# A weight load of the expert stage issued as two transfers: rows 0 to 119 and rows 120 to 127

## The chip, the cores and the metric

The kernel runs on one core of a Trainium2 chip. Its time is the device time in microseconds (us). The median of several runs is taken.

The core has a matrix engine (PE in the profile, TensorE), a vector engine (DVE), a scalar engine (ACT), GpSimd (POOL) and a queue engine (SP). SP only issues transfers here. Sixteen DMA engines carry them. A transfer raises its semaphore by 16 in all when it has landed.

## The reference

A decoder trunk of two layers on 256 tokens of width 1024, in float32. Each layer has a token mixer (attention, pooling, short convolution), a cross-attention and a channel mixer. The channel mixer of the second layer matters here: each token goes to the best 2 of 8 experts.

```python
for e in range(N_EXPERTS):                       # 8 experts, D_FF_EXPERT = 3584
    out = out + gates[:, e:e + 1] * swiglu(xt, w13[e], w2[e])
# swiglu: g, u = split(x @ w13); (silu(g) * u) @ w2
```

An expert's weights are 1024 x 7168 and 3584 x 1024 float32 numbers. They are read once each.

## The kernel before

The expert stage works through items. Item i takes the tokens of one expert (up to 64 in odd items, up to 96 in even ones) through that expert's weights. With these inputs there are eight items; further items, for experts with more tokens, stand in a loop that isn't entered.

The weights of an item come in 42 units (`ITEM_UNITS`), 336 in all. A unit is 128 rows of 2048 float32 numbers, so 8 KB a row and 1 MB a unit. In HBM it is contiguous. Units are laid in a ring of 20 slots (`RING`): six buffers of `raw`, and 14 older tensors that the stage before has finished with, under names such as `slot_bias` and `slot_yT_hi`. Unit number u of the whole stage goes to slot u mod 20. Slot 19 is the tensor `slot_xT_lo`.

SP issues the loads in the order of the units. Before each it waits (`hold`, L402) until PE has read the unit that lay in the slot before, 20 units earlier. `load_unit` (L446) then issues one transfer, which raises `in{slot}` by 16. PE waits in `arrived` (L1907) for `units.landed(u)` on that semaphore, reads the unit with matmuls (`product`, L1860) straight from its slot, and raises `units_read`. The rows of tokens are held as weights of the matmul and the unit is streamed, so a unit costs PE more time in an even item than in an odd one.

Items run in turn: even items with the `mid_up` and `mid_down` forms (L1860, 96 rows, in groups of 32), odd items with `few_up` and `few_down` (64 rows). The last item, number 7, is an odd one. After its last unit come a scaling, the sum back to the tokens (`back`, L1834 and L1835), the final norm, and the output.

An earlier transfer plays a part in the prediction. At L427 four transfers of 32 rows each fill `bias` from the tensor `skew` in HBM.

Of the kernel before, what the change touches and what calls it, by code (L numbers as in the profile page):

```python
# [18 lines left out]
P = 128  # L19
# [28 lines left out]
SPLIT = 3  # L48
RING = 20
OVER_RING = 14  # L50

LAYER_UNITS = 22
DENSE_UNITS = 33
# [124 lines left out]
class Stream:  # L178
# [9 lines left out]
    def landed(self, u):  # L188
        return (self.rounds + ((self.off + u) // RAW + 1)) * 16
# [12 lines left out]
def units_from(first):  # L202
    return Stream(first, first // RAW, first % RAW)
# [6 lines left out]
def layer_stream(l):  # L210
    return units_from(l * (LAYER_UNITS + DENSE_UNITS))

class Units:
# [6 lines left out]
        return (self.off + u) % self.ring  # L221

    def landed(self, u):
        return self.rounds * 16 + ((self.off + u) // self.ring + 1) * 16

    def read(self, u):
        return self.first + (u + 1)
# [5 lines left out]
def item_units(i):  # L233
    u = i * ITEM_UNITS
    return Units(u, u // RING, u % RING, RING)

def over_units(k):

    rounds = (NE * ITEM_UNITS - OVER_RING) // RING + 1  # L240
    return Units(k * ITEM_UNITS + NE * ITEM_UNITS, k * (ITEM_UNITS // OVER_RING) + rounds, 0, OVER_RING)

# [6 lines left out]
def _build(nc, io, ctx):  # L249
# [12 lines left out]
    def sem(name):  # L262
        if name not in sems:
            sems[name] = ctx.enter_context(nc.semaphore(name))
        return sems[name]
# [97 lines left out]
    slots = [raw[:, (MOE_BASE + n) % RAW, :] for n in range(RAW)]  # L363
# [34 lines left out]
    def hold(eng, name, count):  # L398

        eng.wait_ge(sem(name), count)
        eng.sem_inc(sem("held"), 1)  # L402

    @block.sync
    def _(sp):
        def load(st, u, src, width=UNIT):
            hold(sp, f"free{st.slot(u)}", st.freed(u))
            sp.dma_start(raw[:, st.slot(u), 0:width], src).then_inc(sem(f"raw{st.slot(u)}"), 16)

        for t in range(NT):
            sp.dma_start(x_tiles[t], io["x"][0, t * P:(t + 1) * P, :]).then_inc(sem(f"x_in{t}"), 16)
        sp.dma_start(g_row[:, :], io["mix_norm_g"][0].rearrange("(o d) -> o d", o=1).broadcast_to([P, D]))\
            .then_inc(sem("first_gain_in"), 16)
        sp.dma_start(ident, io["mats"][:, 0, :]).then_inc(sem("ident_in"), 16)

        for l in range(DEPTH):
            st = layer_stream(l)
            for u in range(LAYER_UNITS):
                load(st, u, io["layer_units"][l, u])  # L420
                if l == 0 and u == RAW - 1:
                    sp.wait_ge(sem("skew_rows"), 1)
                    sp.dma_start(skew.ap(), skew_rows.unsqueeze(1).broadcast_to([HEADS, SKEW_P, SKEW_W]))\
                        .then_inc(sem("skew_out"), 16)
                    sp.wait_ge(sem("skew_out"), 16)
                    for a in range(0, P, SKEW_P):
                        sp.dma_start(bias[a:a + SKEW_P, :, :],  # L427
                                     bass.AP(skew, P - 1 - a, [[SKEW_W - 1, SKEW_P], [SKEW_P * SKEW_W, HEADS], [1, T]]))\
                            .then_inc(sem("bias_in"), 16)
            if l < 1:  # L430
                for u in range(DENSE_UNITS):
                    load(st, LAYER_UNITS + u, io["dense_units"][u])

        moe = io["moe_units"]
        last = layer_stream(DEPTH - 1)

        def unit_done(u):
            return "unit_used", last.upto(u) + 2 * SPLIT

        room = [(f"free{units_from(MOE_BASE).slot(n)}", units_from(MOE_BASE).freed(n)) for n in range(RAW)]  # L440
        room += [("logits", DEPTH * HEADS), ("xlogits_mm", DEPTH * XHEADS), unit_done(19)]
        room += [unit_done(19)] * 2 + [unit_done(20)] * 2 + [unit_done(21)] * 4 + [("router_mm", 1)] * 3

        def load_unit(units, u, src):
            slot = units.slot(u)
            sp.dma_start(slots[slot], src).then_inc(sem(f"in{slot}"), 16)  # L446

        for u in range(ITEM_UNITS):
            if u < RING:
                hold(sp, *room[u])  # L450
            else:
                hold(sp, "units_read", item_units(0).room(u))
            load_unit(item_units(0), u, moe[u])
        sp.wait_ge(sem("info_ready"), 1)
        n_items = sp.value_load(info[0:1, 0:1], min_val=NE, max_val=ITEMS)
        for i in range(1, NE):
            e = sp.value_load(info[0:1, i + 1:i + 2], min_val=0, max_val=NE - 1)
            for u in range(ITEM_UNITS):
                hold(sp, "units_read", item_units(i).room(u))
                load_unit(item_units(i), u, moe[e * ITEM_UNITS + u])  # L460
        with sp.Fori(0, OVER) as k:
            with sp.If(n_items > k + NE):
                e = sp.value_load(info[0:1, bass.ds(k + (NE + 1), 1)], min_val=0, max_val=NE - 1)
                hold(sp, "units_read", k * ITEM_UNITS + NE * ITEM_UNITS)
                for u in range(ITEM_UNITS):
                    if u >= OVER_RING:
                        hold(sp, "units_read", over_units(k).room(u))
                    load_unit(over_units(k), u, moe[e * ITEM_UNITS + u])
            sp.nop()
        for t in range(NT):  # L470
            for half in range(2):
                s = slice(half * 512, (half + 1) * 512)
                sp.wait_ge(sem("xn_ready"), 4 * (3 * DEPTH + 1) + 2 * t + half + 1)
                sp.dma_start(io["out"][0, t * P:(t + 1) * P, s], xn[:, t, s]).then_inc(sem("out_done"), 16)
        sp.wait_ge(sem("out_done"), 32 * NT)
# [1543 lines left out]
```

## Time and profile before

| | |
|---|---|
| median of 3 runs | 1376.26 us (1376.21 to 1376.49) |
| the profiled execution | 1376.58 us |
| its span, first to last instruction | 1374.7 us |
| PE busy | 1347.6 us, 98% of the span |
| transfers | 444.58 MB, mean 323 GB/s |

The page tells the busy time of each engine, then the span in 40 equal slices, in which a digit is the busy share in tenths. The DMA line is the mean over the 16 DMA engines. A chain follows what ended last back through what released it. Windows give the same for any stretch that one asks for.

### The profile page before, as it was taken

The numbers are of one execution on the slowest core, as the hardware profiler recorded it, in microseconds if no ns is written. First come the engines' busy times: TensorE is split into PE (matmuls) and PEld (weight loads), VectorE is DVE, ScalarE is ACT, GpSimd is POOL, SyncE is SP. The second block draws the span as 40 slices with busy tenths as digits, with TensorE's granted clock in tenths as the row PEclk, the third lists the DMA queues.
The fourth block names the chain that finished last, engine by engine and source line by source line (L and its number), as shares of the span: only waits on it lengthen the run. The fifth ranks groups of instructions, "written<-read, shape, count | busy, mean of one in ns | idle before, by whom it ended". The sixth has DMA issues, their size and how long they took to land.

```text
span 1374.7 us, 29896 instructions
## 1 busy us (share of the span) xinstructions
PE 1347.6 (98%) x13281; PEld 1063.0 (77%) x13281; DVE 411.8 (30%) x761; ACT 321.8 (23%) x587; POOL 13.9 (1%) x27
## 2 busy tenths in 40 slices
PE   9999999999999999999999999999999999999994
PEld 6989888888798888888557888557888557887542
DVE  6677555554747753200100100100100100100102
ACT  6445454443644533000001000001000000000001
POOL 1000000000000000000000000000000000000000
PEclk9999999999999999999999999999999999999998
DMA  8826345555543569999999999999999999999992
GB/s 317 314 96 223 124 169 184 184 187 190 191 154 123 185 250 399 413 378 352 409 421 420 420 419 419 420 421 419 420 420 420 420 421 420 420 420 420 421 420 116
DMA packets 63901, 444.58 MB, mean 323 GB/s; under 512 B 7262, under 2 KB 8686, under 8 KB 10905
## 3 DMA queue, kind: packets, MB, share of 16 engines
q1 hardware_dynamic: 61976, 437.22, 79.7%
q0 software_dynamic: 1792, 5.41, 1.1%
q8 instruction: 106, 1.74, 0.5%
q14 instruction: 27, 0.21, 0.0%
HBM read 441.16 MB, written 1.44 MB: 322 GB/s over the span
## 4 chain that ended last, share of the span: by engine, by line
PE 93%; DVE 3%; DMA 2%; issue 1%; ACT 1%; SPq 0%; DVEq 0%; ACTq 0%
PE bank L1860 52%; PE bank L1440 10%; PE bank L1442 10%; PE bank L1441 10%; PE bank L1824 2%; DMA slot_yT_hi<-in_moe_units 2%; PE bank L1922 2%; PE bank L1834 1%; PE bank L1528 1%; PE bank L1482 1%; PE bank L1835 1%; DVE w_lo L826 1%; PE bank L1649 1%; PE bank L1569 1%; PE bank L1632 1%
## 5 line engine op out<-in xcount | busy, mean ns | idle before, releaser
L1373 DVE TENSOR_TENSOR hidden<-hidden,bank 128x384 f32<-128x384 f32 (+1 forms) x56 | 27.3, 487 | 587.7 <-ACT hidden L786 587.7
L826 DVE TENSOR_TENSOR w_lo<-raw,w_hi 128x1024 fp32r<-128x1024 f32 x154 | 181.1, 1219 | 42.8 <-ACT w_hi L524 41.3
L524 ACT ACTIVATE w_hi<-raw 128x1024 fp32r<-128x1024 f32 x154 | 154.5, 1057 | 40.5 <-PE bank L1442 40.5
L786 ACT ACTIVATE hidden<-bank 128x384 f32<-128x384 f32 (+1 forms) x56 | 24.5, 437 | 365.5 <-PE bank L1860 365.5
L1860 PE MATMUL bank<-raw,mid_x 128*32 128x384 f32 (+1 forms) x1632 | 92.8, 380 | 1.0 <-ACT mid_x L760 1.0
L1860 PEld LDWEIGHTS bank<-raw,mid_x 128*32 128x32 f32 x1632 | 88.7, 110 | 4.5 <-issue 3.1
L779 ACT ACTIVATE hT<-bank 128x384 f32<-128x384 f32 (+1 forms) x56 | 24.5, 437 | 288.5 <-PE bank L1922 288.5
L1440 PE MATMUL bank<-xT_hi,w_hi 128*128 128x256 f32 x320 | 91.8, 287 | 0.0
L1441 PE MATMUL bank<-xT_lo,w_hi 128*128 128x256 f32 x320 | 90.5, 283 | 0.0
L1442 PE MATMUL bank<-xT_hi,w_lo 128*128 128x256 f32 x320 | 90.4, 283 | 0.0
L1440 PE MATMUL bank<-w_hi,xT_hi 128*128 128x512 f32 (+1 forms) x224 | 85.2, 380 | 1.1 <-DVE w_lo L826 0.6
L1442 PE MATMUL bank<-w_hi,xT_lo 128*128 128x512 f32 (+1 forms) x224 | 83.9, 375 | 0.0
L1441 PE MATMUL bank<-w_lo,xT_hi 128*128 128x512 f32 (+1 forms) x224 | 83.8, 374 | 0.0
L1860 PE MATMUL bank<-raw,hT 128*32 128x256 f32 (+2 forms) x792 | 81.8, 476 | 0.0
L1440 PE MATMUL bank<-w_hi,yT_hi 128*128 128x512 f32 x184 | 73.3, 398 | 1.3 <-DVE yT_lo L838 0.8
L1442 PE MATMUL bank<-w_hi,yT_lo 128*128 128x512 f32 x184 | 71.8, 390 | 0.0
L1441 PE MATMUL bank<-w_lo,yT_hi 128*128 128x512 f32 x184 | 71.7, 390 | 0.0
L1860 PEld LDWEIGHTS bank<-raw,hT 128*32 128x32 f32 (+1 forms) x792 | 43.4, 115 | 29.2 <-issue 15.4
L1440 PEld LDWEIGHTS bank<-xT_hi,w_hi 128*128 128x128 f32 x320 | 61.3, 192 | 0.7 <-issue 0.7
L1441 PEld LDWEIGHTS bank<-xT_lo,w_hi 128*128 128x128 f32 x320 | 61.3, 192 | 0.1
L1442 PEld LDWEIGHTS bank<-xT_hi,w_lo 128*128 128x128 f32 x320 | 61.3, 191 | 0.0
L1860 PE MATMUL bank<-raw,few_x 128*64 128x256 f32 x512 | 59.3, 382 | 0.5 <-DMA raw<-in_moe_units 0.5
(326 smaller groups left out, 2100.1 us busy)
## 6 DMA issues: line engine op xcount, KB each, us to landing
raw<-in_moe_units SPq DMA_DIRECT2D x102, 1024.0 KB, 24.9
slot_w_hi<-in_moe_units SPq DMA_DIRECT2D x51, 1024.0 KB, 25.8
slot_w_lo<-in_moe_units SPq DMA_DIRECT2D x51, 1024.0 KB, 26.0
raw<-in_layer_units SPq DMA_DIRECT2D x44, 1024.0 KB, 5.1
raw<-in_dense_units SPq DMA_DIRECT2D x33, 1024.0 KB, 4.9
slot_bias<-in_moe_units SPq DMA_DIRECT2D x17, 1024.0 KB, 26.0
slot_qk<-in_moe_units SPq DMA_DIRECT2D x17, 1024.0 KB, 26.4
slot_memT_lo<-in_moe_units SPq DMA_DIRECT2D x17, 1024.0 KB, 26.7
```

Source lines behind the costliest of these rows:

```text
L524: act.activation(w_hi[:, st.split(u), half, :], raw[:, st.slot(u), half * n:(half + 1) * n], ACT.Copy)\
L779: act.activation(hT[:, j % 2, 0:n, :], bank[3][:, 0:n * P].rearrange("p (b r) -> p b r", b=n), ACT.Copy)\
L786: act.activation(hidden[:, 0:n * P], bank[2][:, 0:n * P], ACT.Silu).then_inc(sem("silu"), 1)
L826: dve.tensor_tensor(w_lo[:, st.split(u), half, :], raw[:, st.slot(u), half * n:(half + 1) * n], w_hi[:, st.split(u), half, :].bitcast(F32) ...
L1373: dve.tensor_tensor(hidden[:, 0:n * P], hidden[:, 0:n * P], bank[j % 2][:, 0:n * P], ALU.mult)\
L1440: pe.matmul(out, hi_l, hi_r, start=start, stop=False, skip_group_check=True)
L1441: pe.matmul(out, hi_l, lo_r, start=False, stop=False, skip_group_check=True)
L1442: return pe.matmul(out, lo_l, hi_r, start=False, stop=stop, skip_group_check=True)
L1482: mm = pe.transpose(bank[b][:, k * P:(k + 1) * P], xn[:, t, a:a + P], ident)
L1824: mm = pe.matmul(out, xn[:, t, k * P:(k + 1) * P], S[:, t, 0:n], start=(t == 0), stop=(t == NT - 1))
L1860: return pe.matmul(out, rows, moving, start=start, stop=stop, skip_group_check=True)
L1922: mm = pe.transpose(bank[3][:, b * P:(b + 1) * P], hidden[:, b * P:(b + 1) * P], ident)
```

## The change

In slot 19 a unit is loaded by two transfers. The first takes rows 0 to 119, the second rows 120 to 127. Each raises `in19` by 16, so `landed` counts 32 for a unit of that slot. The other 19 slots are loaded as before. Bytes, order, buffers and all other instructions stay.

```diff
@@ -48,6 +48,7 @@
 RING = 20
 OVER_RING = 14
+PARTED, PART = RING - 1, 120
@@ -221,7 +222,8 @@
     def landed(self, u):
-        return self.rounds * 16 + ((self.off + u) // self.ring + 1) * 16
+        parts = 2 if self.slot(u) == PARTED else 1
+        return self.rounds * (16 * parts) + ((self.off + u) // self.ring + 1) * (16 * parts)
@@ -443,7 +445,11 @@
         def load_unit(units, u, src):
             slot = units.slot(u)
-            sp.dma_start(slots[slot], src).then_inc(sem(f"in{slot}"), 16)
+            if slot == PARTED:
+                sp.dma_start(slots[slot][0:PART, :], src[0:PART, :]).then_inc(sem(f"in{slot}"), 16)
+                sp.dma_start(slots[slot][PART:P, :], src[PART:P, :]).then_inc(sem(f"in{slot}"), 16)
+            else:
+                sp.dma_start(slots[slot], src).then_inc(sem(f"in{slot}"), 16)
```

## Rows read from the trace of the kernel before

**Rows 1.** Page: engines' busy us and share; DMA by slice.

```profile
PE 1347.6 (98%) x13281; PEld 1063.0 (77%) x13281; DVE 411.8 (30%) x761; ACT 321.8 (23%) x587; POOL 13.9 (1%) x27
...
DMA  8826345555543569999999999999999999999992
```

**Rows 2.** Chain that ended last, from 1318 us: start, us, what.

```profile
1328.16 26.31 DMA slot_yT_hi<-in_moe_units
1354.47 0.04 issue
1354.51 1.96 PE bank L1860 x8
```

**Rows 3.** Timeline, matmuls of the last units: start, us, what, idle before, releaser.

```profile
1329.81 1.95 PE L1860 MATMUL bank<-raw,few_x 128*64 128x256 f32 x16 [0.53 <-DMA raw<-in_moe_units]
...
1354.51 1.94 PE L1860 MATMUL bank<-slot_yT_hi,hT 128*64 128x512 f32 x8 [0.42 <-DMA slot_yT_hi<-in_moe_units]
```

**Rows 4.** Windows: stretch and length, busy of engines, PEclk, DMA share, GB/s.

```profile
656.00:1340.00 684.00, 681.66 (x8120) 493.60 (x8118) 62.93 (x133) 50.14 (x114) 0.00 (x0) 1.00 1.01 420
```

**Rows 5.** Window from the first such wait to the last unit's end.

```profile
1326.00:1356.50 30.50, 25.38 (x164) 10.64 (x158) 0.84 (x2) 1.61 (x6) 0.00 (x0) 1.00 0.70 292
```

**Rows 6.** Windows of the stage's first items.

```profile
580.00:600.00 20.00, 20.00 (x329) 17.51 (x324) 2.57 (x7) 1.29 (x3) 0.00 (x0) 1.00 1.00 389
600.00:620.00 20.00, 20.00 (x343) 18.33 (x338) 0.55 (x1) 1.17 (x3) 0.00 (x0) 1.00 0.99 374
620.00:640.00 20.00, 20.00 (x304) 17.92 (x299) 0.55 (x1) 1.58 (x3) 0.00 (x0) 1.00 0.89 342
640.00:660.00 20.00, 20.00 (x272) 13.97 (x264) 1.57 (x3) 1.85 (x4) 0.00 (x0) 1.00 0.99 371
660.00:680.00 20.00, 20.00 (x160) 11.84 (x158) 2.73 (x6) 1.54 (x4) 0.00 (x0) 1.00 0.99 413
```

**Rows 7.** Windows before and after the first engines have finished.

```profile
1330.00:1340.00 10.00, 8.20 (x52) 3.38 (x51) 0.42 (x1) 0.77 (x2) 0.00 (x0) 1.00 1.02 421
1340.00:1342.00 2.00, 1.70 (x16) 0.86 (x12) 0.00 (x0) 0.00 (x1) 0.00 (x0) 1.00 0.62 258
1342.00:1347.00 5.00, 3.90 (x32) 2.11 (x32) 0.00 (x0) 0.35 (x1) 0.00 (x0) 1.00 0.59 242
1347.00:1352.00 5.00, 4.24 (x18) 1.26 (x18) 0.42 (x1) 0.42 (x2) 0.00 (x0) 1.00 0.51 213
1352.00:1354.40 2.40, 1.94 (x8) 0.57 (x8) 0.00 (x0) 0.00 (x0) 0.00 (x0) 1.00 0.21 89
```

**Rows 8.** SP's transfers into slot 19, to 660 us.

```profile
L446 SPq DMA_DIRECT2D slot_xT_lo<-in_moe_units x3: 327/328/332, 528.5 to 650.1; - x3
```

**Rows 9.** The same from 660 us: ns min/median/max, first and last start.

```profile
L446 SPq DMA_DIRECT2D slot_xT_lo<-in_moe_units x13: 332/1914/3713, 691.5 to 1287.5; - x13
```

**Rows 10.** SP's waits, 540 to 1330 us: total, times, longest.

```profile
SPq L402 <- PE bank L1860: 275.4, 153, 5.9
```

**Rows 11.** Windows in which the 32-row transfers of L427 run, and the raw loads after them.

```profile
33.00:35.00 2.00, 2.00 (x19) 2.00 (x18) 1.34 (x6) 1.03 (x3) 0.00 (x0) 1.00 1.01 247
35.00:37.00 2.00, 2.00 (x19) 2.00 (x18) 1.66 (x4) 1.37 (x2) 0.00 (x0) 1.00 1.17 234
...
38.00:42.00 4.00, 4.00 (x36) 4.00 (x35) 2.83 (x4) 1.09 (x2) 1.56 (x3) 1.00 0.97 394
```

**Rows 12.** Transfers by line: count, KB each, median us from issue to landing.

```profile
bias<-skew SPq DMA_DIRECT2D x4, 256.0 KB, 4.6
...
out<-xn SPq DMA_DIRECT2D x4, 256.0 KB, 2.0
```

## The prediction

> **What bounds the kernel now.** I read the page first. PE is busy for 98% of the span, which looks like a kernel bound by PE; but in the same page the DMA engines are full from the sixteenth slice to the last but one [rows 1]. Two resources are full at once in the expert stage, so the share of busy time can't decide. The chain of waits decides it, for the end: the last unit's transfer is 26.31 us of the chain, it lands at 1354.47, and PE starts on that unit 0.04 us later [rows 2]. The timeline shows that this is no single accident. From 1329.81 on PE needs 1.94 or 1.95 us for a unit and the units start some 2.47 us apart: 11 starts from 1329.81 to 1354.51, so ten gaps in 24.70 us. Nearly all of them are released by a DMA [rows 3]. In this last stretch PE is busy for 25.38 of 30.50 us, so it idles for 5.1 us [rows 5].
>
> How long has the DMA side been the limit? From 656 to 1340 us the engines' share is 1.01 and they move 420 GB/s [rows 4]: a unit of 1.049 MB each 2.50 us. Nothing idles there. PE was not waiting before 1326, since the ring had given it a lead; but a microsecond that the transfers lose after 656 is not won back by anybody, and comes out as a microsecond at 1354.47, because the last stretch of PE has no reserve left. From 580 to 680 us it is otherwise: 389, 374, 342, 371 and 413 GB/s in five windows of 20 us [rows 6]. Against 420 these are 1.5, 2.2, 3.7, 2.3 and 0.3 us of unused capacity, 10 us together. Here SP waited for room, and a lost microsecond is absorbed.
>
> **What the change does.** Slot 19 takes 16 of the 336 units (one in 21). Three are issued by 650.1 us [rows 8], 13 from 691.5 to 1287.5 us [rows 9]. The first three fall before or into the unused 10 us and are costed at nothing; if that cover weren't there they would cost what the others do. (The third meets only the last 2 us of it and may leave 1 us.) So every price is multiplied by 13.
>
> *The second issue on SP.* It takes 0.33 us when the queue has room [rows 8], and most issues take 1.9 us from 691.5 on [rows 9], as SP is held up by a queue that is full. SP waits for room for 275.4 us besides [rows 10]. Thirteen issues of 0.33 us, 4.3 us in all, lie in that wait; some 26 us of transfers are queued ahead [rows 2], so no engine runs dry for them. Cost: nothing. Behind the issue wait the loads of the next units, which have the same cover. PE's wait for 32 instead of 16 is the same instruction.
>
> *The 120-row transfer.* The trace has none. Bounds: at the least it moves at the full 420 GB/s, 2.34 us of the 2.50, no loss. At the other end stands the one place where transfers cover part of the partitions: the four loads of `bias`, 32 rows each. There the engines are as full as ever (share 1.01 and 1.17) and move only 247 and 234 GB/s; a little later whole 128-row loads are back at 394 [rows 11]. Nor is it the size of a piece alone: 256 KB to `bias` take 4.6 us, 256 KB of `out`, over all 128 rows, take 2.0 [rows 12]. The mean of the two rates is 240 GB/s, and a unit at this rate takes 4.36 us instead of 2.50: 1.86 us lost. The busy time goes up and the rate down, which is what engines look like that get in each other's way where they write. Why should 120 rows be like 32? A whole unit is dealt out so that 16 engines run at full rate beside each other. 120 rows can't be dealt out in the same way to 16 engines in whole rows of equal number (7.5 each), so some other dealing must be used, and nothing makes sure that it is as free of collisions. I take the row of the 32-row transfers, 1.86 us, and keep 0 as the low end.
>
> *The 8-row transfer.* 64 KB. An engine's share of a unit is 8 rows in 2.50 us, 0.31 us a row. If the eight rows are spread with no collision, the transfer costs 0.16 us (64 KB at 420 GB/s); if they are written one after the other, 2.5 us. I take 0.8 us, nearer to the low end: several engines will share it, but if 32 neighbouring rows already collide [rows 11], eight do so more.
>
> *Sum.* 13 x (1.86 + 0.8) = 34.6 us. The path behind it (last unit, scaling, `back`, norm, output; 20 us) doesn't change. The profiled execution stands at 1376.58, 0.3 above the median of the runs. 1376.3 + 34.6 = 1411 us.
>
> **A rule beside the row.** The slow rate of the 32-row loads in [rows 11] is the row. The Trainium skill ("SBUF — State Buffer", section "Door 1: The DMA port swizzle") says that DMA bandwidth depends on how many of 16 SBUF ports the partitions reach, and that partitions 0 to 63 reach only eight. 
>
> **Rivals.**
>
> *Hidden (22%).* The engines don't end together. Their share is 1.02 up to 1340 and then 0.62, 0.59, 0.51 and 0.21 [rows 7]: about half of them have finished all their work 13 us before the last lands. If 120 rows are dealt out without collisions and the eight extra rows fall on engines of this early half, they cost 13 x 0.31 = 4 us where 13 us are free. Time 1376, within 0.2%. Against it: [rows 11]. It decides where the 120-row transfer loses less than 0.2 us. This is the rival of the other side.
>
> *One row too many (10%).* No collisions, but the eight rows fall on the late half: 13 x 0.31 = 4.1 us, 1380.4. No row tells on which half they fall. It has less than the hidden rival, since an end that is 4 us later also needs the loaded engine to be among the very last.
>
> *Faster (4%).* If one engine gets nothing of the 120 rows and it alone is the last, the end comes earlier. The most that this could give is PE's idle time in the last stretch, 5.1 us less 0.4 for the last wait: 1371.6. The skill speaks for it ("DMA: Bandwidth & Descriptors", section "Latency and other measured facts": engines 7 and 15 are usually slower in traces). Against it is the decline in [rows 7]: a share of 0.51 from 1347 to 1352 is eight engines, and 0.21 in the last 2.4 us is more than three on average. With one taken away the next ends less than 1 us sooner.
>
> *Much slower (6%).* Neighbouring rows go to neighbouring engines one by one, so that four share a place: three times 2.5 us more a load, 13 x 7.5 = 98 us, 1474.
>
> The forecast has the remaining 58%. Its own range: 13 x (1.86 + 0.16) = 26 us at the low end; at the high end 13 x (1.86 + 2.5) = 57, of which I take up to 13 x (2.5 + 1.7) = 55: 1402 to 1431. That the split isn't carried out is no rival: 16 loads of `slot_xT_lo` ran.
>
> **How the numbers follow.** The time is the likeliest case's, 1411. The range for eight in ten must reach down to the hidden case, so from 1375.6 to 1431; it leaves out the much slower case, the faster one, and the outer ends of the forecast. A measurement of this kernel can tell 0.2%, 2.8 us, from no change. Slower by more than that: 58 + 10 + 6 = 74%. Within: 22%. Faster: 4%.
>
> **What the profile after would show.** Windows from 700 to 1300 below 420 GB/s while the DMA share stays at 1.0 or above: with 34.6 us lost in some 700, a mean near 400. Waits of PE for DMA well before 1326, in the odd items, whose units PE reads faster than 2.5 us each. Transfers into `slot_xT_lo` landing later than their neighbours by more than 1 us. If instead the rate stays at 420 and the share declines as in [rows 7], the 120-row transfer is free of collisions and the hidden case holds. The second issue should take 0.3 to 2 us on SP and no wait should end at it. The prediction is wrong if 120 rows are dealt out as cleanly as 128, and its size is wrong if a collision costs the neighbouring loads too.

## The result and the profile after

The changed kernel takes 1480.75 us in the median (1477.90 to 1485.68, 4 runs) against 1376.24 (1376.08 to 1376.49). The ratio is 1.0763, with a 95% interval from 1.0729 to 1.0797: slower by 104.5 us, three times the 34.6 us that were forecast and outside the range. The profiled execution took 1485.68 us.

The page after, the rows that answer to [rows 1]:

```profile
PE 1376.0 (93%) x13281; PEld 1062.3 (72%) x13281; DVE 411.7 (28%) x761; ACT 321.9 (22%) x587; POOL 13.9 (1%) x27
...
DMA  8734455544535699999999999999999999999991
GB/s 312 299 140 159 144 210 191 204 145 168 189 114 186 258 376 417 377 348 420 375 367 405 368 341 412 345 339 413 332 347 398 316 375 364 320 394 324 364 371 59
```

The digits of the DMA line are still 9 from slice to slice, while the rate beneath them goes up and down between 316 and 420. Engines that are busy all the time move less. Windows of the kernel after; the first answers to [rows 4] and [rows 5], the others cut out single falls of the rate:

```profile
656.00:1340.00 684.00, 625.00 (x7481) 450.36 (x7479) 54.21 (x116) 44.21 (x99) 0.00 (x0) 0.98 1.01 368
...
755.00:775.00 20.00, 20.00 (x323) 17.54 (x319) 2.35 (x5) 0.98 (x2) 0.00 (x0) 1.00 1.02 324
920.00:925.00 5.00, 4.01 (x20) 1.17 (x18) 0.00 (x0) 0.00 (x0) 0.00 (x0) 1.00 1.01 421
925.00:945.00 20.00, 9.63 (x72) 4.68 (x68) 0.42 (x1) 0.77 (x2) 0.00 (x0) 1.00 1.02 268
945.00:950.00 5.00, 4.44 (x17) 1.80 (x18) 0.00 (x0) 0.00 (x0) 0.00 (x0) 0.66 1.01 418
1330.00:1375.00 45.00, 39.32 (x431) 24.84 (x429) 2.42 (x5) 3.50 (x8) 0.00 (x0) 0.92 1.00 330
```

The last two numbers of a row are the share of busy DMA engines and the GB/s. Over 684 us the share is the 1.01 of before and the rate 368 instead of 420: 684 x (1 - 368/420) = 85 us of transfer lost. The loss comes in bursts. At 920 the rate is 421; from 925 to 945 it is 268; at 945 it is back. That burst loses 20 x (1 - 268/421) = 7.3 us, and a whole unit takes 2.5. An earlier one, from 755, loses 4.6 us, a late one, from 1330, 9.7 us over 45 us. So a burst is longer than one load's transfer, and it grows in the course of the run. Two windows of equal length, around the split loads of units 79 and 279, show the growth:

```profile
672.00:720.00 48.00, 48.00 (x357) 26.67 (x356) 6.30 (x14) 3.07 (x8) 0.00 (x0) 1.00 1.01 385
1262.00:1310.00 48.00, 44.97 (x707) 37.50 (x699) 5.08 (x11) 2.46 (x5) 0.00 (x0) 1.00 1.01 335
```

They lose 48 x (1 - 385/421) = 4.1 us and 48 x (1 - 335/421) = 9.8 us. The kernel before moves 421 and 420 GB/s in the same windows.

The timeline of the matmuls in the burst from 925, PE alone; it answers to [rows 3]:

```profile
932.66 1.95 PE L1866 MATMUL bank<-slot_yT_lo,few_x 128*64 128x256 f32 x16 [2.48 <-DMA slot_yT_lo<-in_moe_units]
936.68 1.95 PE L1866 MATMUL bank<-slot_memT_hi,few_x 128*64 128x256 f32 x16 [2.08 <-DMA slot_memT_hi<-in_moe_units]
940.47 1.94 PE L1866 MATMUL bank<-slot_xT_hi,hT 128*64 128x512 f32 x8 [1.83 <-DMA slot_xT_hi<-in_moe_units]
```

These three units stand in slots 16, 17 and 18, before the split one. They aren't split, and they come 4.0 and 3.8 us apart instead of 2.5. The loads beside the split load are slow as well.

The split load on SP, in answer to [rows 8] and [rows 9] (L449 issues the 120 rows, L450 the 8):

```profile
L449 SPq DMA_DIRECT2D slot_xT_lo<-in_moe_units x16: 350/1942/6051, 527.6 to 1388.6; - x16
L450 SPq DMA_DIRECT2D slot_xT_lo<-in_moe_units x16: 283/1935/1988, 528.0 to 1390.7; - x16
```

SP's waits from 540 to 1430 us, in answer to [rows 10]:

```profile
SPq L404 <- PE bank L1866: 129.6, 68, 5.9
```

Both issues have the longer time of a full queue in the median, and SP still waits for room for 129.6 us: it isn't SP that is late. The chain's last transfer, in answer to [rows 2]:

```profile
1436.87 26.61 DMA slot_yT_hi<-in_moe_units
```

A window before it lands, in answer to [rows 7]:

```profile
1452.00:1463.00 11.00, 9.18 (x54) 3.38 (x50) 0.42 (x1) 0.77 (x2) 0.00 (x0) 1.00 0.11 45
```

The end hangs on the transfers as it did before. In the last 11 us the share is 0.11, not two engines of 16. The engines are further apart at the end than in [rows 7]: the semaphore of this last unit takes its 16 steps, one for each engine, in 18.5 us, where before the change it takes them in 13.8.

### The profile page after: what moved, and what is told of

Read it like the earlier page. It is cut to its first block, busy times and chain, and to the rows that moved or that the text cites. A ratio compares the mean times of both kernels' runs of the same rounds, so it can differ in the third digit from the quotient of the medians.

```text
span 1483.9 us, 29940 instructions
## 1 busy us (share of the span) xinstructions
PE 1376.0 (93%) x13281; PEld 1062.3 (72%) x13281; DVE 411.7 (28%) x761; ACT 321.9 (22%) x587; POOL 13.9 (1%) x27
## 4 chain that ended last, share of the span: by engine, by line
PE 60%; SPq 25%; DMA 9%; issue 3%; DVE 3%; ACT 1%; DVEq 0%; ACTq 0%
PE bank L1866 24%; SPq L452 23%; PE bank L1446 9%; PE bank L1448 9%; PE bank L1447 9%; DMA raw<-in_moe_units 3%; DMA slot_xT_lo<-in_moe_units 2%; DMA slot_memT_hi<-in_moe_units 2%; DMA slot_yT_hi<-in_moe_units 2%; PE bank L1830 2%; SPq L449 1%; PE bank L1928 1%; PE bank L1488 1%; SPq L450 1%; PE bank L1534 1%
```

## The experiments

Two theories stood against each other at first. A: a transfer that doesn't cover all 128 rows deals its rows to the engines in another way than a whole unit does, and engines then hold each other up where they write. B: the second issue, or the counting to 32, costs. C, a form of A, blames the 8 rows and not the 120. Where neither an interval nor a number of runs stands beside a time below, the kernel was executed once.

### Two transfers by columns

```diff
-                sp.dma_start(slots[slot][0:PART, :], src[0:PART, :])...
-                sp.dma_start(slots[slot][PART:P, :], src[PART:P, :])...
+                sp.dma_start(slots[slot][:, 0:half], src[:, 0:half])...
+                sp.dma_start(slots[slot][:, half:], src[:, half:])...
```

> The load of slot 19 is again two transfers with the same counting, but each takes all 128 rows and half of the columns. Theory A (transfers that don't deal their rows to the engines as a whole unit does collide with the others): no collision here, so the time stays within 0.3% of before, 1374 to 1380 us. Theory B (a second issue in a full queue, or the counting to 32, is what costs): as slow as the change, near 1480 us.

Measured: 1377.09 us against 1375.74, ratio 1.0009 (1.0000 to 1.0019). The window of the whole stage:

```profile
656.00:1340.00 684.00, 681.66 (x8120) 493.46 (x8118) 62.50 (x133) 50.18 (x114) 0.00 (x0) 1.00 1.01 419
```

B falls. Sixteen more issues, the count of 32 and rows cut to 4 KB together cost some 1.4 us, within 0.2%; the interval reaches down to no difference.

### Rows 0 to 119 alone

```diff
-                sp.dma_start(slots[slot][PART:P, :], src[PART:P, :])...
```

`landed` counts 16 a load again, and the first load of slot 19 is whole (`...`, not shown). The other 15 units of the slot lack their last 8 rows.

> Slot 19 gets rows 0 to 119 by one transfer and rows 120 to 127 not at all, except in its first load, which is whole (so part of the weights is stale; 15 loads of 16 are concerned). Theory A with the 120-row transfer as the culprit: most of the 104 us stays, 1450 to 1480 us, and the rate falls to some 240 to 300 GB/s for ten or more microseconds at each. Theory C (the 8-row transfer is the culprit): 1370 to 1380 us. Theory B: the same, since there is one issue.

Measured: 1476.80 us, so 101 us of the 104.5 are still there. The windows at one burst:

```profile
918.00:922.00 4.00, 3.39 (x24) 1.40 (x20) 0.00 (x0) 0.03 (x1) 0.00 (x0) 1.00 1.01 420
922.00:940.00 18.00, 10.52 (x56) 4.77 (x56) 0.42 (x1) 0.74 (x2) 0.00 (x0) 0.81 1.02 235
942.00:952.00 10.00, 10.00 (x74) 7.37 (x72) 0.00 (x0) 1.26 (x3) 0.00 (x0) 0.85 1.02 423
```

The burst, here at unit 159, is the same one without the 8-row transfers, and with one issue for each load. C falls.

### Rows 120 to 127 alone

```diff
-                sp.dma_start(slots[slot][0:PART, :], src[0:PART, :])...
```

The count and the first load are as in the run before; 15 units lack 120 rows.

> Slot 19 gets rows 120 to 127 alone, except in its first load, which is whole (120 rows of 15 units are stale). 35 us of transfer time are left out, so the time can fall to what PE needs, 1371 us. Theory A with the 120-row transfer as the culprit: 1371 to 1373 us, and the rate at these loads doesn't fall by half. Theory C: 50 us or more must remain above 1371 after 35 are saved, so 1400 us or more.

Measured: 1366.80 us, lower than expected. PE no longer waits for any transfer in the stage, so this is the time that PE needs, 9 us below before and not 5. Two of the 9 lie behind the last unit: between the last `y_lo` and `back` the chain shows 3.40 us where it shows 5.43 before. The prediction took that path as fixed. Where the rest of the difference lies wasn't looked for. The run speaks against C, but weakly on the size: 13 loads leave out 13 x 2.34 = 30.4 us of transfers and the time falls by 9, so a cost of up to (30.4 - 9) / 13 = 1.6 us for each load would be hidden. In its windows at one of these loads the rate is 374 and 380 GB/s for ten microseconds, with the share near 1:

```profile
795.00:800.00 5.00, 5.00 (x73) 3.57 (x65) 0.55 (x1) 0.49 (x1) 0.00 (x0) 1.00 1.06 374
800.00:805.00 5.00, 5.00 (x84) 4.30 (x83) 2.02 (x6) 0.49 (x1) 0.00 (x0) 1.00 0.97 380
805.00:810.00 5.00, 5.00 (x99) 5.00 (x95) 0.00 (x0) 0.00 (x0) 0.00 (x0) 1.00 1.01 421
```

That is 5 x (1 - 374/421) + 5 x (1 - 380/421) = 1.0 us lost, near the 0.8 us of the prediction for the 8 rows. Between the change and the 120 rows alone there are 4 us, 0.3 for each of the 13 loads.

### Halves of 64 rows

```diff
-PARTED, PART = RING - 1, 120
+PARTED, PART = RING - 1, 64
```

> Two transfers as in the change, but rows 0 to 63 and 64 to 127, so both have a number of rows that all 16 engines can share equally (4 each). Theory A1 (collisions come from which rows an engine writes, not from how many engines take part): still slow, 1420 to 1500 us. Theory A2 (what costs is that 120 rows go to fewer than 16 engines and leave them uneven): within 0.3% of before, 1374 to 1380 us.

Measured: 1496.31 us, 16 us more than the change. 64 rows can be shared equally by 16 engines and still cost no less. It is not the uneven number 120, nor an engine that is left out; A1 holds.

The traces show how many engines take part, as each raises the semaphore by a step of its own when its share has landed. A whole load of slot 19 shows 16 steps and two transfers of 64 rows 32. The change shows 25 a load and the 120 rows alone 16, and the 8 rows alone 9. In the emptied queue (next section) one step of each of the two transfers comes within 0.6 us of its issue and 23 come when data has landed: 15 engines for the 120 rows, 8 for the 8 rows, and two steps that stand for the engines without a share.

### What the burst is made of

The size was still open: 8.0 us for each of 13 loads (104.5 / 13), where a load that moves at 240 GB/s loses 1.9 us. Theory S: the 120-row transfer slows itself by a few microseconds, and the rest comes from engines that stand at different loads, where those in the split load write beside those that are in a whole one. Theory I: it is slow by 8 us by itself.

The first pair empties the queue around the load of slot 19. Its edit, the same in both kernels but for a count of 32 instead of 16 in slot 19, with the whole load and with the split one:

```diff
         def load_unit(units, u, src):
             slot = units.slot(u)
+            if slot == RING - 1:
+                drained(units, u - 1)        # waits for in0 ... in19 of all older loads
...
+                if item_units(i).slot(u) == 0:
+                    drained(item_units(i), u - 1)
```

> As before (one whole transfer for slot 19), but SP waits until all older loads have landed before it issues the load of slot 19, and until that has landed before it issues the next. Both theories: each drain costs some 4 us of empty engines (issue to first byte, and the landing of a lone load, about 5 us for 2.5 us of data), 13 x 4 = 50 us at most; 1400 to 1430 us. It is the measure for the next run. A lone whole load lands in 4.7 to 5.5 us.

> The same emptied queue, with the load of slot 19 as rows 0 to 119 and 120 to 127, so no other load is in flight and all engines start on it together. Theory S (the 120-row transfer slows itself by 2.5 us, and the rest of the 8 us a load comes from engines that stand at different loads and write into each other's ports): 13 to 16 x 2.5 us over the run before, 30 to 45 us more. Theory I (the 120-row transfer by itself takes 8 us too much, whoever is beside it): 100 to 130 us more.

Measured: 1457.25 us with the whole load, more than the 1430 expected (the queue is emptied 16 times for 81 us: 5 us a time, or 6.2 if only 13 of them count, and not 4). With the split load 1504.76 us, 47.5 more. SP's timeline with the whole load, then with the split one, in each case the load of slot 19 and the next issue, which waits for its landing:

```profile
936.22 0.33 SPq L456 DMA_DIRECT2D slot_xT_lo<-in_moe_units  x1
941.19 0.93 SPq L456 DMA_DIRECT2D raw<-in_moe_units  x2
```

```profile
957.70 0.35 SPq L459 DMA_DIRECT2D slot_xT_lo<-in_moe_units  x1
958.24 0.29 SPq L460 DMA_DIRECT2D slot_xT_lo<-in_moe_units  x1
965.63 0.36 SPq L462 DMA_DIRECT2D raw<-in_moe_units  x1
```

From issue to next issue it is 4.97 us whole and 7.93 us split. By itself the split costs 2.96 us, and 16 x 2.96 = 47 us is what the two times differ by. Theory I falls; the difference is a little above the 30 to 45 us of theory S. It isn't the second issue either: while a whole load is alone an engine writes a row of 8 KB in 0.31 us in the median, and while the split one is alone in 0.60. These 3.0 us are near the 2.66 of the prediction, which has priced a split load that stands alone.

The second pair splits a single load, unit 79 or unit 299, in an otherwise unchanged kernel:

```diff
-            if slot == PARTED:
+            if slot == PARTED and units.first + u == 79:      # 299 in the other
```

`landed` counts the 16 of the second transfer from that unit on.

> Only one of the 16 loads of slot 19 is split: unit 79, about 690 us into the run, when the landings of the loads still take only 15 us and the engines stand close together. Theory S: the fall of the rate there loses 3 to 4.5 us, and the time is 1379 to 1381 us. Theory I: 7 to 8 us, 1383 to 1385 us.

> Only unit 299 is split, issued at about 1236 us, when by the trace of before about half of the engines are some 13 us ahead of the others. Theory S: the low rate lasts as long as the engines are apart, 13 us or more, and 6 to 8 us are lost; 1382 to 1385 us, and 2.5 us or more above the run with unit 79. Theory I: the same time as that run, within 1 us.

Measured: 1380.03 us for unit 79, ratio 1.0030 (1.0018 to 1.0041), and 1383.64 us for unit 299, ratio 1.0055 (1.0033 to 1.0078). The same two transfers cost 3.7 us early and 7.3 us late. The intervals of the two ratios overlap, but the windows of each profile show the burst itself. Unit 79:

```profile
690.00:700.00 10.00, 10.00 (x75) 5.07 (x73) 1.65 (x5) 0.69 (x2) 0.00 (x0) 1.00 1.01 421
700.00:712.00 12.00, 12.00 (x96) 6.54 (x92) 0.42 (x1) 0.84 (x3) 0.00 (x0) 1.00 1.02 301
712.00:722.00 10.00, 10.00 (x77) 6.24 (x74) 0.42 (x1) 0.39 (x1) 0.00 (x0) 1.00 1.01 417
```

Unit 299:

```profile
1235.00:1245.00 10.00, 10.00 (x141) 8.36 (x130) 0.56 (x1) 0.49 (x1) 0.00 (x0) 1.00 1.02 421
1247.00:1272.00 25.00, 25.00 (x369) 19.12 (x362) 1.58 (x3) 2.34 (x5) 0.00 (x0) 1.00 1.02 299
1272.00:1282.00 10.00, 10.00 (x94) 6.42 (x92) 0.42 (x1) 0.77 (x2) 0.00 (x0) 1.00 1.01 419
```

The mean rate over the burst is much the same, 301 and 299 GB/s, but over 12 us in one and over 25 in the other: 3.4 and 7.2 us lost. The long one isn't even: slices of 5 us show 282, 316, 378, 254 and 262 GB/s. Each loss appears whole in the time of the run. PE is busy all through both windows, so the loss is only paid at the end, as the prediction said of this stage. What differs between the places is how far the engines are apart, and the semaphores show it. In the kernel before, the 16 steps of unit 78 come within 2.1 us and those of unit 298 within 12.9 us, seven engines early and eight late. In the run with unit 299 split the load just ahead of it takes its steps from 1248.5 to 1268.2 us, and the low rate lasts from 1247 to 1272: a stretch for the early group, a stretch for the late one, and 378 GB/s between.

The third pair limits that distance. SP issues a load when the load three places before it has landed:

```diff
         def load_unit(units, u, src):
             slot = units.slot(u)
+            v = units.first + u - 3
+            if units.ring == RING and v >= 0:
+                sp.wait_ge(sem(f"in{v % RING}"), 16 * (v // RING + 1) * ...)   # 2 for slot 19 when split
```

> As before, all loads whole, but SP issues a load of the expert stage only when the load three places earlier has landed, so no engine can be more than three loads (7.5 us) ahead of the last one, against the 13 us that the trace of before shows. Both theories: nothing much changes, 1376 to 1390 us; it is the measure for the next run.

> The change, with the same rule of three loads in flight. Theory S (the low rate lasts while the engines stand at different loads): the loss of a split load stays at 3 to 5 us all through the run, so 45 to 65 us above the run before, against 104 us without the rule. Theory I (the number of loads in flight doesn't matter): 100 us or more above it.

Measured: 1381.90 us with whole loads (10 runs, from 1377.05 to 1389.89), 1444.13 us with split ones (two runs, 1442.39 and 1445.86). The window of the stage, whole and split:

```profile
656.00:1340.00 684.00, 679.01 (x8086) 490.84 (x8082) 61.96 (x131) 49.76 (x113) 0.00 (x0) 1.00 1.01 413
656.00:1340.00 684.00, 648.90 (x7773) 468.45 (x7769) 58.58 (x125) 46.68 (x105) 0.00 (x0) 0.99 1.01 380
```

The difference of the times is 62 us against 104.5 without the rule. The change with three loads in flight is 37 us faster than the change as it is. The rule did what it was meant to: from unit 78 on, the steps of a whole load never lie more than 5.5 us apart, where they lie up to 13 apart in the kernel before and up to 30 in the changed one. And the losses no longer grow: windows of 48 us around the 13 loads lose 5.0 us in the mean in the first seven and 5.0 in the last six. Theory S holds. For the 13 loads that have no cover it is 4.8 us each. Some 40% of what the change costs is gone when the engines are held together.

### All loads split

```diff
-            if slot == PARTED:
+            if True:
```

`landed` counts 32 in every slot.

> All 336 loads of the stage are split at row 120, not one in 20. Theory P (engines that write rows of one place at once get half of the rate each, whoever is beside them): the rate of the whole stage is near that of the 32-row transfers, 220 to 270 GB/s, and the time 1900 to 2150 us. Theory M (only the mixing of a split load with whole ones costs): with nothing to mix the rate is near 400 GB/s, and the time below 1450 us.

Measured: 2099.88 us. Its windows:

```profile
656.00:1340.00 684.00, 448.77 (x4103) 268.42 (x4106) 31.14 (x66) 26.90 (x61) 0.00 (x0) 0.86 0.93 229
1340.00:2000.00 660.00, 433.18 (x4198) 269.98 (x4189) 31.45 (x66) 24.22 (x54) 0.00 (x0) 0.86 0.92 218
```

Theory P holds and theory M falls. With nothing whole to mix with the stage moves 218 to 229 GB/s, near the rate of the 32-row transfers in [rows 11] and about half of 420. A row of 8 KB takes an engine 0.54 us in the median, against 0.31 before. So the collision is among the engines of a split load too; being mixed with whole ones makes it longer.

## Why the prediction was right or wrong

**The bound** was right. The transfers are the limit from about 656 us on, and what they lose comes out at the end. The first two split loads are hidden, as forecast: the steps of unit 56, on the semaphore of its slot, come at 646 us in the mean, before and after. The third is not: those of unit 76 come at 700.8 us where they came at 698.4, so it leaves 2.4 us where the sum has nothing and the text at most 1. Past the cover, units 79 and 299 split alone lost 3.4 and 7.2 us in their windows and 3.7 and 7.3 us in their times, at about 700 and 1250 us into runs of 1380.

**The second issue** was costed at nothing. By columns it is some 1.4 us for 16.

**The 120-row transfer** was read from the 32-row ones with the right outcome: engines full, rate at some 240 GB/s. The windows of the burst show 268 and 235, all loads split 218 to 229. But the rows didn't carry as much as the text took from them. The 32-row transfers move in packets of 1 KB (962 of the 1023 packets from 31 to 37 us), the loads of the stage in packets of 8 KB, so their low rate had a second possible cause. The comparison with `out` in [rows 12] doesn't exclude it, as `out` is a store to HBM in pieces of 2 KB. It was the runs with 64 rows and with all loads split, both with rows of 8 KB, that did.

**The 8-row transfer** was put at 0.8 us. Without it the change still takes 1476.80 us, 4 us less, and the run with the 8 rows alone shows 1.0 us at one load. The sum also counts its 64 KB twice, as the 1.86 us are for a whole unit; that is 0.16 us a load.

**The step that failed** is the sum's price of a split load, "The mean of the two rates is 240 GB/s, and a unit at this rate takes 4.36 us instead of 2.50: 1.86 us lost." It applies the low rate to the split load's own megabyte. That holds when the load is alone: 2.66 us were forecast and 3.0 measured in the emptied queue. In the full queue the low rate lasts until the last engine has left the split load, 12 us early in the run and 20 to 45 us later. At unit 159 this can be followed: one engine is past the load ahead of it at 916.6 us, at 925.0 the next one is, the last at 940.3, and the split load has landed at 945.5; the rate is low from 925 to 945. So a load costs 4.1 us at unit 79 and 9.8 us at unit 279, and 8.0 us on average if all 104.5 us are put on 13 loads. (Windows of 48 us around each of the 13 add up to 98 us.) The term had to be a stretch of time times the part of the rate that is lost in it, 0.29 for each of the two loads split alone and 0.36 at unit 159. For the length of the stretch [rows 7] gave a hint: engines that finish 13 us apart. I read that row as cover for the hidden rival, and it bears on the length of the collision. The text closed with "its size is wrong if a collision costs the neighbouring loads too", which is what happened, but neither the sum nor the range held it.

**The rivals.** Hidden, one row too many and faster are out. Much slower named 1474 us and came near the time for another reason: it priced the split load itself at 7.5 us more, and alone it takes 3.0 us more.

**The pages.** The rule of ports in the Trainium skill ("SBUF — State Buffer", "Door 1: The DMA port swizzle") fits the runs: 64 rows cost no less than 120 do, and all loads split run at about half rate. The other rule, of the largest k that divides the rows, agrees with the steps of the semaphores: 15 engines and 8. My estimate from the pages, 44 us, had the same fault as the sum. The remark on engines 7 and 15 was no argument for the faster rival: the same row of the Trainium skill ("DMA: Bandwidth & Descriptors", "Latency and other measured facts") calls its likely cause specific to transfers issued from GpSimd, and these are issued from SP.

**Open.** Which rows each engine gets wasn't seen; that they meet at ports is the page's account and not shown here by more than the halved rates. The growth of the bursts has two sources, and their shares are settled only in part. Engines drift apart in the kernel before as well, and the single split load at unit 299 already costs 7.2 us. But the split loads drive them apart much faster: the steps of unit 138 come within 5.1 us before the change and within 20 after it, and within 23 with halves of 64 rows, where no engine is left out. From there on they stay between 20 and 30 us apart while the loss still grows, which isn't explained. With three loads in flight 4.8 us are left, above the 3.0 of a load that stands alone.

## What to carry to other kernels

A transfer that doesn't take all 128 rows of a tile can cost more than its own time when the queue is full: here 4 to 10 us for each one amid loads of 2.5 us. Split by columns where a split is needed, which was free within 0.2%. To price a disturbance of a shared, full resource, ask how long its users stay in it, not how many bytes it has: users that run apart stretch it.

## What the runs showed of the hardware that was not expected

The share of busy DMA engines does not see a collision: it was 1.02 at 268 GB/s and at 421 GB/s. The rate beside it does.

The sixteen engines drift apart under a full queue. Before the change the steps of a load come within 2 us at 700 us and within 13 at 1310; after it not two of 16 engines are busy in the last 11 us. A possible source of the drift before the change, argued and not tested, is the fetching of instructions: packets of 16 KB that take an engine 1.0 to 1.1 us each and come 7 to 19 us apart. Between 700 and 1310 us there are 60 of them. Shared by eight engines that would be 8 us each, and in that time eight engines fall 11 us behind the others. Keeping three loads in flight instead of about ten (26 us from issue to landing, 2.5 us a load) cost some 6 us with whole loads (ratio 1.0044, 1.0026 to 1.0062) and saved 37 us with split ones.

PE's granted clock, whose two levels are 2.4 and 1.2 GHz, was 0.66 of full speed in the 5 us after the burst at 925 us, a mean of both levels. PE had been idle for half of the burst. With all loads split it was 0.86 in both windows of the stage. As the transfers set the end, what the clock cost can't be read from these runs.
